# The sparse-attention and recurrence mixer of a two-block model in another order of columns and heads

## What is computed

```python
h = rmsnorm(x, mix_pre_g)
q, k_cmp, v_cmp, k_sel, v_sel, k_win, v_win, gates, xb, yb = split(h @ w_in)   # 4632 columns
kc, vc = compress(k_cmp, pos_k, k_w1, k_w2), compress(v_cmp, pos_v, v_w1, v_w2)
# compress: 15 windows of 32 positions x 128 -> gelu(. @ w1) @ w2, for 2 kv groups
o = g0 * attend(q, kc, vc) + g1 * attend(q, k_sel, v_sel) + g2 * attend(q, k_win, v_win)   # 8 heads of 128
# rec: conv of 4 taps, two block-diagonal gates r, i, h_t = a_t * h_(t-1) + u_t, times gelu(yb)
y = concat(rmsnorm(o, attn_out_g), rmsnorm(rec, rec_out_g))
x = x + rmsnorm(y @ w_out, mix_post_g)
```

## Time and profile before

| | before |
|---|---|
| median of 3 runs | 3042.7 us (3040.08 to 3045.18) |
| profiled execution: its time, its span | 3044.29 us, 3042.5 us |
| PE busy | 2920.7 us, 96% |
| PE weight loads | 2419.7 us, 80% |
| DVE, ACT, POOL busy | 1728.0 us (57%), 1298.8 us (43%), 14.2 us |
| mean granted PE clock | 0.981 |
| DMA | 530.60 MB, 174 GB/s on average |

### The profile page before, as it was taken

The page is one execution under the profiler, slowest core; times in us unless marked ns, Lnnn a source line. Parts: engine busy times, 40 slices in busy tenths (PEclk is TensorE's granted clock), DMA queues, the critical chain, the costliest instruction groups (busy, mean ns, idle before and its releaser), DMA issues.

```text
span 3042.5 us, 33344 instructions
## 1 busy us (share of the span) xinstructions
PE 2920.7 (96%) x13590; PEld 2419.7 (80%) x13590; DVE 1728.0 (57%) x1622; ACT 1298.8 (43%) x1340; POOL 14.2 (0%) x17
## 2 busy tenths in 40 slices
PE   8999899999989999999999999777999999999997
PEld 7878788878878888888888788665788888888876
DVE  5468755445465555555555744764655555555574
ACT  5444444344444433333433545443443333333453
POOL 0000000000000000000000000000000000000000
PEclk9999999999999999999999999997999999999999
DMA  6545255544445555555555554412565555555544
GB/s 237 194 147 183 95 183 180 193 165 165 134 140 186 196 192 193 193 190 188 188 193 192 168 186 166 165 56 97 169 208 193 193 189 188 188 193 191 189 170 141
DMA packets 275615, 530.60 MB, mean 174 GB/s; under 512 B 8640, under 2 KB 30288, under 8 KB 274752
## 3 DMA queue, kind: packets, MB, share of 16 engines
q1 hardware_dynamic: 275088, 528.25, 51.8%
q0 software_dynamic: 432, 0.99, 0.1%
HBM read 527.12 MB, written 2.10 MB: 174 GB/s over the span
## 4 chain that ended last, share of the span: by engine, by line
PE 64%; DVE 4%; ACT 2%; issue 1%; DMA 0%; SPq 0%; DVEq 0%; ACTq 0%
PE ps L594 19%; PE ps L596 19%; PE ps L595 19%; PE ps L612 1%; PE ps L613 1%; PE ps L614 1%; PE ps L674 1%; DVE w_lo L1615 1%; PE ps L760 0%; ACT w_hi L1101 0%; PE ps L1058 0%; PE ps L704 0%; PE ps L780 0%; DVE st L1848 0%; DMA raw<-in_w_in 0%
## 5 line engine op out<-in xcount | busy, mean ns | idle before, releaser
L1615 DVE TENSOR_TENSOR w_lo<-raw,w_hi 128x2048 fp32r<-128x2048 f32 (+2 forms) x503 | 1126.8, 2244 | 833.2 <-ACT w_hi L1101 831.6
L1101 ACT ACTIVATE w_hi<-raw 128x2048 fp32r<-128x2048 f32 (+2 forms) x503 | 942.0, 1878 | 1028.0 <-DMA raw<-in_ff_w_down 320.5
L594 PE MATMUL ps<-w_hi,x_hi 128*128 128x512 f32 (+3 forms) x3176 | 1234.0, 389 | 11.9 <-DVE w_lo L1615 11.9
L596 PE MATMUL ps<-w_hi,x_lo 128*128 128x512 f32 (+3 forms) x3176 | 1225.0, 386 | 0.0
L595 PE MATMUL ps<-w_lo,x_hi 128*128 128x512 f32 (+3 forms) x3176 | 1224.3, 385 | 0.0
L594 PEld LDWEIGHTS ps<-w_hi,x_hi 128*128 128x128 f32 x3176 | 599.3, 189 | 133.6 <-DVE w_lo L1615 11.3
L596 PEld LDWEIGHTS ps<-w_hi,x_lo 128*128 128x128 f32 x3176 | 598.3, 188 | 119.3
L595 PEld LDWEIGHTS ps<-w_lo,x_hi 128*128 128x128 f32 x3176 | 599.3, 189 | 116.1
L594 PE MATMUL ps<-w_hi,h_hi 128*128 128x512 f32 x652 | 254.8, 391 | 2.0 <-DVE h_lo L2331 2.0
L595 PE MATMUL ps<-w_lo,h_hi 128*128 128x512 f32 x652 | 254.5, 390 | 0.0
L596 PE MATMUL ps<-w_hi,h_lo 128*128 128x512 f32 x652 | 254.3, 390 | 0.0
(11 more groups left out here) (290 smaller groups left out, 1542.3 us busy)
## 6 DMA issues: line engine op xcount, KB each, us to landing
raw<-in_w_in SPq DMA_DIRECT2D x143, 1024.0 KB, 5.0
raw<-in_ff_w_gate SPq DMA_DIRECT2D x88, 1024.0 KB, 5.0
raw<-in_ff_w_up SPq DMA_DIRECT2D x88, 1024.0 KB, 5.0
raw<-in_ff_w_down SPq DMA_DIRECT2D x88, 1024.0 KB, 5.1
raw<-in_w_out SPq DMA_DIRECT2D x48, 1024.0 KB, 5.0
raw<-in_w_ple_gate SPq DMA_DIRECT2D x16, 1024.0 KB, 5.1
z<-in_rows SPq DMA_DIRECT2D x5, 1024.0 KB, 7.2
raw<-in_w_in SPq DMA_DIRECT2D x8, 536.0 KB, 3.6
```

Source lines behind the costliest of these rows:

```text
L594: nc.tensor.matmul(o, x[0][:, k0 + c, s], hi[:, c, 0:width], start=first and c == 0, stop=False)
L596: m = nc.tensor.matmul(o, x[1][:, k0 + c, s], hi[:, c, 0:width], start=False, stop=last and c == n - 1)
L1101: nc.scalar.activation(landed_part(w_hi, u, j), landed_part(raw, u, j), ACT.Copy).then_inc(hi_ready, 1)
L1615: V.tensor_tensor(landed_part(w_lo, u, j), landed_part(raw, u, j), landed_part(w_hi, u, j).bitcast(F32), ALU.subtract).then_inc(parts_read ...
```

## The change

The same 64 units and the same columns of `w_in` are computed in another order:

1. The compressed keys and values (512 columns) come first, then 352 columns with the head gates and a part of the recurrent x. Then five blocks are taken in turn, unit by unit: 348 columns, compression of k, 348 columns, compression of v, 512 columns of y. Then the rest of y, half of q, window k/v, selected k/v, and the other half of q.
2. Heads 32 to 47 now go four window heads and four selected heads for each kv group, with `halves_beside` units beside them: 16 half units, that is the second half of q (4 units), block 2 of the output matrix over the recurrent chunks 8 and 12 (2 units, kept in `out_part`), and block 0 over the same chunks (2 units).
3. The output matrix is taken recurrent chunks first; only the attention chunks wait for the attention.
4. The compressed attention is done for all heads at once: value rows repeated and masked into a block-diagonal matrix `cmp_vs`, two transposes and four matmuls of 128x512.
5. The attention norm sums its squares in four parts (`attention_squares`), three of them before the last head is done. The rotations are spread. POOL no longer clears `work`, and the gain row is loaded into `z`.

```diff
-    MIX_REC = plan(t["w_in_2"], ZG, [BW] * 3 + [268, 268])
-    MIX_QKV = plan(t["w_in_2"], 0, [BW] * 5)
-    CMP = plan_other(4)
-    plan_other(4)
-    MIX_OUT = plan(t["w_out_2"], 0, [BW] * 4)
+    MIX_COMPRESSED = plan(t["w_in_2"], ZKC, [BW])
+    MIX_REC = plan(t["w_in_2"], ZG, [352])
+    MIX_TOGETHER = in_turn([(t["w_in_2"], ZG + 352, 348, quarter(range(0, KC, UC))), (None, 0, 0, [None] * 4),
+                            (t["w_in_2"], ZG + 700, 348, quarter(range(0, KC, UC))), (None, 0, 0, [None] * 4),
+                            (t["w_in_2"], ZY, BW, quarter(range(0, KC, UC)))],
+                           [0, 0, 1, 0, 1, 0, 1, 2, 1, 2, 2, 3, 2, 3, 4, 3, 4, 3, 4, 4])
+    CMP = (MIX_TOGETHER + 1, MIX_TOGETHER + 3)
+    MIX_Y = plan(t["w_in_2"], ZY + BW, [BW])
+    MIX_Q = plan(t["w_in_2"], ZQ, [BW])
+    MIX_WINDOW = plan(t["w_in_2"], ZKW, [BW])
+    MIX_SELECTED = plan(t["w_in_2"], ZKS, [BW])
+    MIX_Q2 = plan(t["w_in_2"], ZQ + BW, [BW])
+    OUT_PART = in_turn([(t["w_out_2"], 2 * BW, BW, quarter((8, 12)))])
+    MIX_OUT = in_turn([(t["w_out_2"], c * BW, BW, quarter((8, 12, 0, 4))) for c in range(2)], [0, 0, 1, 1, 0, 0, 1, 1])
...
-        beside = [1, 0] * 8 + [3] + [4] * 3 + [3] * 3 + [4] + [2] * 7 + [1] + [0] * 16
+        halves_beside = [2, 2, 1, 1, 1, 1, 0, 0] + [1] * 7 + [0]
...
+            def advance_halves(n):
+                for _ in range(halves_beside[n - 32]):
+                    if at[0] == first_unit[OUT_PART]:
+                        pe.wait_ge(made["rec_lo"], 1)
+                    advance_half(halves[0] % 2)
+                    halves[0] += 1
...
-            advance(11)
+            pe.wait_ge(made["cmp_added"], 2)
+            advance(1)
...
+            for s in range(4):
+                turn_attention(s)
+                if s == 1:
+                    pe.wait_ge(st_done, turned_before["attn"] + 2)
+                    advance(1)
+            pe.wait_ge(st_done, turned_before["attn"] + 4)
+            until(end_unit[MIX_OUT + 3] - 1)
```

More of the change, by code:

```diff
@@ L441, in load_block, with load_units @@
                          w[k0 * P:(k0 + n) * P, c0:c0 + width].rearrange("(k p) n -> p k n", p=P), u < RAW)
+            def load_units(u0, u1):
+                for u in range(u0, u1):
+                    b, place = block_of[u]
+                    _, w, c0, width, units = blocks[b]
+                    j = u % RAW
+                    if b in CMP:
+                        w1 = t[("cmp_k_w1", "cmp_v_w1")[CMP.index(b)]]
+                        load(u, j, raw[:, j, :].rearrange("p (l n) -> p l n", l=8),
+                             w1[place * 1024:(place + 1) * 1024, :].rearrange("(l p) n -> p l n", p=P))
+                    else:
+                        k0, n = units[place]
+                        load(u, j, slot(j, n, width),
+                             w[k0 * P:(k0 + n) * P, c0:c0 + width].rearrange("(k p) n -> p k n", p=P))
             def load_run(b, count):
@@ L962, in _, with until @@
             tiled_first_block("mix", of_res, updated(0), next_by_tile)
-            advance(18)
-            all_drained(pe, MIX_QKV)
-            pe.wait_ge(st_done, turned_before["mix"] + 8)
+            def until(u):
+                while at[0] < u:
+                    b, place = block_of[at[0]]
+                    if b not in CMP:
+                        advance(1)
+                        continue
+                    m = CMP.index(b)
+                    j = at[0] % RAW
+                    if place == 0:
+                        pe.wait_ge(made["cmp_lo"], m + 1)
+                        pe.wait_ge(drained[pair_of[b]], drains_before[b])
+                    pe.wait_ge(parts_ready, at[0] + 1)
+                    hi, lo = (w[:, j, :].rearrange("p (l n) -> p l n", l=8) for w in (w_hi, w_lo))
+                    x = cmp_parts[m]
+                    for l in range(8):
+                        c = (8 * place + l) * 32
+                        o = ps[0:32, 2 * pair_of[b], 0:256]
+                        nc.tensor.matmul(o, x[0][:, c:c + 32], hi[:, l, :], start=place + l == 0, stop=False)
+                        nc.tensor.matmul(o, x[0][:, c:c + 32], lo[:, l, :], start=False, stop=False)
+                        i = nc.tensor.matmul(o, x[1][:, c:c + 32], hi[:, l, :], start=False,
+                                             stop=place == 3 and l == 7)
+                    i.then_inc(parts_used, 1)
+                    at[0] += 1
             def turn_channels(c0):
@@ L1040, in _ @@
[L1040 to L1041 removed]
+            for k in range(2):
+                i = nc.tensor.matmul(ps[:, 7, P:2 * P], cmp_hidT_heads[:, k, :], cmp_w2[:, 1, k, :],
+                                     start=k == 0, stop=k == 1)
+            i.then_inc(made["cmp_kv_made"], 1)
+            until(first_unit[MIX_SELECTED] + 1)
+            pe.wait_ge(made["rec_out_squared"], 1)
+            for b in range(LB):
+                i = nc.tensor.matmul(ps[:, 4, 0:SEQ], ones[:], by_block(r2)[:, b, :], start=b == 0, stop=b == LB - 1)
@@ L1138, in drain @@
                     i.then_inc(drained[pair_of[b]], 1)
+                elif kind == "part":
+                    for tt in range(NT):
+                        i = nc.scalar.activation(out_part[:, tt], summed(b)[:, tt], ACT.Copy)
+                    i.then_inc(drained[pair_of[b]], 1)
+                elif kind == "output" and b == MIX_OUT + 2:
+                    act.wait_ge(made["part_added"], 1)
+                    tail_sums([out_part[:, tt] for tt in range(NT)], 2)
                 elif kind == "output":
```

607 lines of the change are left out of this document (362 added, 245 removed).

## The result

The changed kernel takes 3002.3 us (median of 4 runs, 3002.1 to 3003.4) against 3041.8 of the kernel before on the same chip (4 runs, 3040.1 to 3045.2): a ratio of 0.9869, 95% interval 0.9852 to 0.9887. It is 39.6 us faster. The forecast was 2990, with 2975 to 3005 around it: the sign and the range held, the size fell 12 us short.

What follows compares the result with a forecast made beforehand. TensorE, busy 96% of the span, was taken as the bound, so only its idle or slow-clocked time could be won. 23.1 + 17.9 + 11.6 - 0.4 = 52.2 us saved gave 2990 us, 8 in 10 within 2975 to 3005.

Steps and rivals of the forecast that it cites:

- Part 1: New unit order ahead of the heads: 33.9 us lost before, 10.8 left, so 23.1 us saved.
- 0.9 where the gate matrices are loaded: Ahead of the heads: a TensorE wait of 0.9 us left where gate matrices are loaded between units.
- the 1.3 at ScalarE's root: Ahead of the heads: 1.3 us lost where ScalarE's root of 2048 columns precedes copies of the compression's hidden rows.
- The 6.7 at the first compression unit: Ahead of the heads: TensorE idle 6.7 us for the compression sums' low half, with 1.9 us of lower clock behind.
- Parts 2 and 3: Half units beside the heads, 17.9 us saved; compressed attention for all heads at once, 11.6 us saved.
- the rival of the splits in the head order: Each of 8 units inside the heads comes 2 us late, losing 16 us: 3006 us, chance 0.16.
- Part 4: Attention's norm with two units between its transposes: waits of about 6.2 and 2.1 us, costing 0.4 us overall.
- fewer waits: Rival: stalls at the first compression unit and in the norm don't appear, 16.7 us less: 2973 us, chance 0.09.
- The lower clock through all the heads: Rival: TensorE stays at half speed through the heads, 68 us more: 3058 us, chance 0.02.

Runs made afterwards that it cites:

- the later constant: Changed kernel with ScalarE computing the recurrence's constant (a table load and two small instructions) two splits later: 3000.6 us, ratio 0.9866.
- the quarters: Gate matrices loaded in four pieces with a weight load between them, against the changed kernel; only in combined kernels, first timed at 2986.2 and 2983.1 us.
- In turn: Changed kernel plus low halves first, later constant, other bank pair, later attention wait and compressed transposes, gate pieces; five blocks still taken unit by unit: 2983.1 us.
- apart: Changed kernel with the same combined edits, but the five blocks one behind the other: 2986.2 us, ratio 0.9817.
- the norm's new order: Combined-edits kernel with blocks one behind the other, plus ScalarE's and VectorE's splits moved behind their work on the attention's first pair: 2980.7 us, ratio 0.9801.

## Why the prediction was right, and where it was 11 us too large

The stage came out at 423.3 where the forecast had 412. Term by term:

- **Part 1, forecast 23.1, measured 18.8** (274.4 less 21.8 is 252.6; now 233.8). The terms that were mis-sized: first "0.9 where the gate matrices are loaded", for which no row was given. The unit there waits 2.3, and 1.6 of lower clock follow, 3.9 together, 3.0 too little. I had taken the DMA engines' mean share of 0.52 as room. Where the loads fall the engines move 350 GB/s without a gap, and that row of the mean does not show it. Second, the sum took all 33.9 us of loss of before as gone but for 10.8. In the first 10 us of the mixer the granted clock is 0.83 in both kernels, 1.7 us that the change does not touch, and a wait of 0.8 for ScalarE's rotation (L1137) stands ahead of the heads. Against these, the 1.3 at ScalarE's root did not come. With 0.4 more at the first compression unit (6.8 and 2.2, forecast 6.7 and 1.9) this makes 4.6, against 4.3 by the stretch.
- **The 6.7 at the first compression unit was partly luck.** The chain was walked as 8.6 and 1.9 us against one unit of 3.8. In the trace it takes 14.4 from the end of the transposes (1760.9) to the first compression matmul (1775.3), since the sums start only behind a split, and two units stand beside it, 7.6. Both numbers were short by about 3.8, so the difference came out right. The main cause, the split ahead of the low half, was named rightly, and the runs show it.

The first 10 us before and after, then the lines of the after kernel at the two places:

```profile
1718.20:1728.20 10.00, 9.99 (x41) 8.19 (x42) 8.57 (x13) 6.01 (x12) 0.00 (x0) 0.83 0.07 12
1718.20:1728.20 10.00, 9.94 (x41) 8.18 (x42) 8.57 (x13) 5.96 (x12) 0.00 (x0) 0.83 0.06 10
...
1759.88 1.04 PE L1103 MATMUL ps<-ident,z 128*128 128x128 f32 x8
...
1763.72 2.29 DVE L1770 TENSOR_TENSOR w_lo<-raw,w_hi 128x2048 fp32r<-128x2048 f32 x1 [4.19 <-ACT w_hi L1209]
...
1816.87 0.31 PE L1077 MATMUL ps<-w_hi,value_parts 128*32 128x256 f32 x1 [2.29 <-DVE w_lo L1770]
```

- **Parts 2 and 3, forecast 29.5, measured 26.6** (85.7 from the first head to the last sum before, now 102.6 less 43.5 of halves). The heads with a half came at 5.13 us each where 5.05 was taken (TensorE's half units from 2002.86 to 2023.38, four heads; VectorE's copies there come unevenly, 5.23 in the mean of three gaps). I had 8.0 for heads 38 and 39 together; they take 11.6 (TensorE's turns at 1990.47 and 2002.02), with 2.6 idle in one wait and much of the rest at the lower clock: 0.69 over the 8 us from 1992.1 on. That is the rival of the splits in the head order, but at one place, not at eight. The compressed attention has no large miss: 3.9 idle, and two pairs of matmuls at 1.7 us each, where 3.3 was put for all four.

```profile
L1995 DVE COPY work<-ps x4: 551/554/558, 2002.7 to 2018.4; 128x384 f32<-128x384 f32 x4
...
1990.47 0.38 PE L803 MATMUL ps<-ident,z 128*128 128x128 f32 x2
...
1993.41 0.49 PE L846 MATMUL ps<-z,work 128*128 128x128 f32 x2 [2.56 <-DVE work L1995]
...
2002.02 0.61 PE L803 MATMUL ps<-ident,z 128*128 128x128 f32 x4
2002.86 0.50 PE L650 MATMUL ps<-w_hi,x_hi 128*128 128x512 f32 x1 [0.23 <-DVE x_lo L2159]
...
2023.38 0.48 PE L650 MATMUL ps<-w_hi,x_hi 128*128 128x512 f32 x1
```

- **Part 4, forecast a cost of 0.4, measured 2.5** (25.3 less two units is 14.4, and 1.8 of clock behind, against 13.7). The waits were right; the lower clock came twice, in unit 53 (2.5) and in unit 54 (1.8), and I had counted it once.
- **Not forecast, 1.8:** the wait of 2.0 us for the bank pair.

4.3, 2.9, 2.1 and 1.8 make 11.1. The other 1.5 of the 12.6 between 52.2 and 39.6 are between medians and the profiled executions (3044.3 to 3002.1 is 42.2, the medians 39.6) and outside the stage.

The rivals: splits late at all 8 units did not happen; fewer waits did not either. The lower clock through all the heads did not come: it is 0.95 over their whole stretch, and 1.00 with TensorE busy 19.91 of 20 us where half units stand beside them. The Trainium skill's rule in "TensorE: Matmul & The Clock Gate", section "A second HAM failure mode: psum-queue depth-cycling", does not describe these heads; the clock fell at heads 38 and 39, which have no half unit. The rule of table sets in the Trainium skill ("ScalarE: Activation LUTs", section "Table sets: the hidden batching unit") agrees in kind: a load of 1.28 stands in front of the constant's exponential, and the later constant gave 1.7 us of wait.

Left open: what the quarters are worth. In turn 1.0 us of wait is left behind the gate loads, apart 1.2 and 2.1, and no run moves the four pieces alone.

## What to carry to other kernels

An order that was written for the bound engine must be walked on the others too: the two longest waits here, 6.8 and 6.6 us, were work standing behind a split for whose input the engine sat idle (4.00 and 2.87 us on VectorE), and those of 2.6 and 3.9 were work behind a split that was itself on time. When loads are moved, look in the trace of before for what they cost where they stood. Do not judge interleaving by a version that carries such a stall; remove the stall, then compare, and compare the stretch as well as the whole. When a block is added to a rotation of two buffers, look who takes the next turn: parity moves.

## What the runs showed of the hardware

The granted clock around gaps of TensorE, in the changed kernel (us, busy, clock, DMA share, GB/s): the gap of 6.8 us and behind it, then the gap of 6.6 and behind it.

```profile
1769.00:1775.00 6.00, 0.00 (x0) 0.86 0.49 145
1775.40:1777.40 2.00, 2.00 (x10) 0.50 0.00 0
...
2061.90:2068.60 6.70, 0.17 (x2) 0.62 0.43 153
2068.70:2070.70 2.00, 2.00 (x5) 0.50 0.00 0
```

0.50 is the level of 1.2 GHz: behind each of these gaps the next unit starts at it and costs 2.2 and 2.5 us more, about a third on top of the gap. Over the runs a gap of 6.6 us cost 2.1 to 2.8 more, and one of 4.9 us 1.5, 2.8 and 2.9.

Behind shorter gaps the same length comes out both ways. In the changed kernel the unit behind the wait of 2.29 at 1816.87 took 4.36 us in place of 2.80, with TensorE busy for the 39 us ahead of it, and the unit behind the wait of 2.34 at 2079.97 took 7.2 in place of 5.44. With the norm's new order the unit behind the same wait of 2.34 took 5.6, and in the kernel before one behind 2.37 took 5.8. The unit of 7.2 had the gap of 6.6 some 11 us ahead of it, the one of 4.36 had none, so what stood idle shortly before is not the whole reason; it stays open. Behind waits of 1.0 to 1.6 us ahead of the heads at most 0.3 us was added. So in these runs a wait of 2 to 4 us came with 0.1 to 1.8 us more, and one of over 4 with 1.4 to 2.9, and I had not expected it to be so much.
